# VectorE makes both low halves of a weight unit from the fourth z unit on; GpSimd keeps the inputs of the scan and the roots

## The reference, cut to what matters

```python
proj = h @ w_in
z, xBC, dt_raw = split(proj, [D_INNER, D_INNER + CONV_DIM])   # z: 2048 wide
xBC = silu(causal_depthwise_conv(xBC)); xs, Bm, Cm = split(xBC)
dt = softplus(dt_raw + dt_bias); cum = cumsum(dt * A)         # per head, 32 heads
L = exp(where(causal, cum[t] - cum[s], -inf))
y = sum_s (C_t . B_s) * L[t, s] * dt_s * x_s + D_skip * x     # 4 groups of 8 heads
y = y * silu(z); y = y * rsqrt(mean(y * y) per group + eps) * g_out
h = h + y @ w_out                                             # w_out: 2048 x 1024
```

## Time and profile before

| what | before |
|---|---|
| median of three runs | 934.71 us |
| the profiled execution | 935.1 us |
| its span, first to last instruction | 933.3 us |
| TensorE products busy | 911.1 us (98%) |
| VectorE busy | 607.2 us (65%) |
| ScalarE busy | 473.8 us (51%) |
| GpSimd busy | 123.1 us (13%), 100 instructions |
| second halves: VectorE L1744, GpSimd L2436 | 106, 21 |
| mean granted TensorE clock | 0.998 |

### The profile page before, as it was taken

How to read it: one execution, slowest core, us unless ns; L and a number is a source line. 1 busy time by engine, 2 the same in 40 slices (tenths; PEclk the granted TensorE clock), 3 DMA queues, 4 the chain that set the end, 5 groups by cost and what they waited for, 6 DMA issues and landing times.

```text
span 933.3 us, 13488 instructions
## 1 busy us (share of the span) xinstructions
PE 911.1 (98%) x4978; PEld 767.0 (82%) x4978; DVE 607.2 (65%) x1071; ACT 473.8 (51%) x764; POOL 123.1 (13%) x100
## 2 busy tenths in 40 slices
PE   9999999999999999999999999999999999999996
PEld 7999878889888869887888888877978788888885
DVE  4898677676668585767664545567486965555445
ACT  5855757466686444762543443325574354334330
POOL 5643863102000010002000000000001100000001
PEclk9999999999999999999999999999999999999999
DMA  9655232663533128232475555544432265555521
GB/s 351 231 183 169 95 124 86 224 227 137 188 128 136 57 68 338 91 112 116 156 261 182 180 201 199 172 150 163 154 136 91 95 226 213 175 193 180 184 87 45
DMA packets 22235, 151.72 MB, mean 163 GB/s; under 512 B 2592, under 2 KB 2976, under 8 KB 4256
## 3 DMA queue, kind: packets, MB, share of 16 engines
q1 hardware_dynamic: 20160, 142.62, 42.8%
q10 hardware_dynamic: 2016, 8.29, 2.3%
HBM read 149.85 MB, written 1.05 MB: 162 GB/s over the span
## 4 chain that ended last, share of the span: by engine, by line
PE 85%; DVE 8%; issue 3%; ACT 3%; POOL 1%; POOLq 0%; DVEq 0%; ACTq 0%
PE ps L492 15%; PE ps L494 15%; PE ps L498 15%; PE ps L1091 5%; PE ps L523 3%; PE ps L527 3%; PE ps L525 3%; PE ps L767 2%; PE ps L769 2%; PE ps L768 2%; PE ps L543 2%; PE ps L1109 2%; PE ps L663 2%; PE ps L666 1%; PE ps L665 1%
## 5 line engine op out<-in xcount | busy, mean ns | idle before, releaser
L1273 ACT CAST whi<-raw 128x2048 fp32r<-128x2048 f32 (+1 forms) x127 | 241.3, 1906 | 145.2 <-PE ps L498 112.6
L1738 DVE TENSOR_TENSOR wlo<-raw,whi 128x1024 fp32r<-128x1024 f32 x127 | 167.3, 1317 | 139.2 <-ACT whi L1273 138.8
L492 PE MATMUL ps<-whi,ahi 128*128 128x512 f32 (+2 forms) x448 | 173.6, 388 | 0.8 <-issue 0.6
L494 PE MATMUL ps<-wlo,ahi 128*128 128x512 f32 (+2 forms) x448 | 171.7, 383 | 0.0
L498 PE MATMUL ps<-whi,alo 128*128 128x512 f32 (+2 forms) x448 | 170.8, 384 | 0.0
L1744 DVE TENSOR_TENSOR wlo<-raw,whi 128x1024 fp32r<-128x1024 f32 x106 | 129.2, 1219 | 0.0
L492 PEld LDWEIGHTS ps<-whi,ahi 128*128 128x128 f32 x448 | 84.1, 188 | 18.5 <-issue 2.5
L498 PEld LDWEIGHTS ps<-whi,alo 128*128 128x128 f32 x448 | 84.1, 188 | 16.5
L494 PEld LDWEIGHTS ps<-wlo,ahi 128*128 128x128 f32 x448 | 84.2, 188 | 16.3 <-issue 0.5
L523 PE MATMUL ps<-ahi,whi 128*128 128x256 f32 x256 | 73.2, 286 | 0.0
L525 PE MATMUL ps<-alo,whi 128*128 128x256 f32 x256 | 72.4, 283 | 0.0
(11 more groups left out here) (282 smaller groups left out, 1710.2 us busy)
## 6 DMA issues: line engine op xcount, KB each, us to landing
raw<-in_wstream SPq DMA_DIRECT2D x134, 1024.0 KB, 4.8
par<-in_params ACTq DMA_DIRECT2D x5, 1024.0 KB, 4.8
tab<-in_tables ACTq DMA_DIRECT2D x1, 1370.0 KB, 9.0
res<-in_x SPq DMA_DIRECT2D x2, 512.0 KB, 4.6
out<-res SPq DMA_DIRECT2D x4, 256.0 KB, 2.0
par<-in_params ACTq DMA_DIRECT2D x1, 512.0 KB, 3.7
arena<-in_wf ACTq DMA_DIRECT2D x2, 256.0 KB, 5.1
arena<-in_wsmall ACTq DMA_DIRECT2D x1, 256.0 KB, 8.6
```

The costliest lines, as they stand in the source:

```text
L492: pe.matmul(banks[b][:, 0:cw], h_, wh[:, i, c], start=st, stop=False, skip_group_check=True)
L494: pe.matmul(banks[b][:, 0:cw], h_, wl[:, i, c], start=False, stop=False, skip_group_check=True)
L1273: act.copy(whi[:, u % SPL, c], raw[:, u % RAW, c]).then_inc(w_hi, 1)
L1738: dve.tensor_tensor(wlo[:, u % SPL, c], raw[:, u % RAW, c], whi[:, u % SPL, c].bitcast(F32), ALU.subtract).then_inc(w_lo_v, 1)
```

## The change

One line. `WHOLE_FROM` goes from unit 21 to unit 15:

```diff
-WHOLE_FROM = ("ssm_out", 1)
+WHOLE_FROM = ("z", 3)
```

## The result

The changed kernel takes 943.45 us (median of four runs, 943.40 to 945.03) against 934.75 for the kernel before (median of its four): 8.7 us or 0.97% longer, ratio 1.0097 with a 95% interval of 1.0086 to 1.0109. The forecast was 942.3, in a range of 938.3 to 944.3. The profiled execution took 943.4 us with a span of 941.6 (before 935.1 and 933.3).

What follows compares the result with a forecast made beforehand. TensorE was taken to bound the kernel, each stop in the scan lasting to the end; 1.11 + 2.61 + 1.6 + 1.14 + 1.14 = 7.6 us on 934.71 gave 942.3 us, range 938.3 to 944.3.

Steps and rivals of the forecast that it cites:

- place 1: Units 15 and 16, ahead of `bound(2)`: VectorE 4.0 us late, 2.9 hidden by TensorE's lead, +1.11 us.
- GpSimd's relief: GpSimd loses some 14 us of work; claimed worth nothing by itself, as TensorE waits for none of its halves.
- The lock goes to and fro: VectorE's SBUF halves and GpSimd's operations exclude each other and alternate; chance 0.68, 942.3 us.
- The rival of unparted halves: VectorE makes its two halves without GpSimd between: 938.6 us; chance 0.23, including parted at some places only.
- place 2: Unit 17 at pair 4, meeting GpSimd's inputs of group 2: TensorE restarts at 121.72 instead of 118.00, +2.61 us here.
- place 5: Unit 20 at pair 15, ahead of `y_out(3)`, gate products and norms before TensorE's turn of y: +1.14 us.
- place 3: Unit 18 at pair 8, meeting GpSimd's inputs of group 3: `mixw(9)` 1.93 us late, +1.6 goes on.
- place 4: Unit 19 at pair 11: `mixw(12)` comes one half later and TensorE waited there already, +1.14 us.
- about 1.1 near 111: TensorE's wait at L689 for `mixw` near 111 us in the changed profile, named beforehand as about 1.1 us.
- near 133: TensorE's wait at L689 for `mixw` near 133 us in the changed profile, named beforehand as 1.7 us.
- The clock: Rival: TensorE's clock falls to 1.2 GHz behind new stalls; two such places give some 947 us; chance 0.04, another late wait included.

Runs made afterwards that it cites:

- the spread halves: Changed kernel with units 17 to 19 cut into single halves put where VectorE waits for exponentials; 936.04 us.
- filled: Changed kernel with 11 unused products added on TensorE at p = 5, ahead of the L689 that waits longest; 942.02 us.
- l17: Kernel before, with both halves of units 17 to 20 on VectorE, units 15 and 16 shared as before; 940.71 us.
- l18: Kernel before, with both halves of units 18 to 20 on VectorE; 938.65 us.
- lock: Changed kernel with GpSimd's inputs of groups 1, 2 and 3 held back until VectorE made both halves of units 16, 17 and 18; 938.79 us.
- l19: Kernel before, with both halves of units 19 and 20 on VectorE; 937.07 us.

## Why the prediction was right, and what it missed

*TensorE bounds, and a wait in the scan stays to the end.* Right: the lateness of 8.69 us at the turn of y is still 8.3 at the end, and the 0.4 between them is found in other kernels' traces too.

*The order of the scan is a chain through VectorE and ScalarE with TensorE beside it.* Right: at place 1 TensorE's lead hid 2.9 of 4.0 us, as forecast, at the other four nearly all of VectorE's lateness came through, and the spread halves, on the same engine in the same number, cost almost nothing at places 2 to 4.

*GpSimd's relief is worth nothing, its earlier inputs cost.* Right: with its inputs held back the time fell by 4.7 us.

*The lock goes to and fro, operation by operation.* Right in every turn seen; a half took 2.06 us wherever a whole GpSimd operation got in ahead of it. By the rule of the Trainium skill that I cited for it (SBUF — State Buffer, Who interferes with whom) the loser blocks for the whole instruction, and the trace agrees: 2.06 is 1.22 and most of a GpSimd operation of 1.04. The rival of unparted halves gave 938.6, and the kernel in which they are nearly all unparted took 938.79. (A side remark of the prediction is not right for the kernel before: GpSimd's inputs of group 2 start there at 116.21, right behind its own half, and wait for no `y_out`; in the changed kernel they do, for 6.99 us.)

*Terms.* Place 1 1.07 for 1.11, place 2 2.62 for 2.61, place 5 1.13 for 1.14. The forecast for place 3 was a little short (1.6, measured 1.74 in "filled") and that for place 4 a little long (1.14, measured 0.93); together 2.74 for 2.67. At place 3 I had gone by the chain and not by TensorE: `mixw(9)` at 128.83 would have let it restart at 129.56 and it started at 129.74, so it was itself the later one by 0.18, and 1.93 less 0.18 is 1.75. Of the waits named beforehand, "about 1.1 near 111" was the lateness and not the wait (0.51), and "near 133" does not follow from the prediction's own sum, which gives 129.74 + 5.3 = 135.0.

*The clock.* This was the term missing from the forecast, as I had put it aside as a rival with a chance of 0.04, two such places and 947 us. It came at one place and cost 1.2 to 1.4 us, which is the whole of the forecast's error of 1.15: the wait of 2.7 us was foreseen, and that no row showed what such a wait does was said, but from waits of 1.0 us at full clock I took it as nearly excluded. Without it ("filled") the time is 942.02, against 942.3. That 943.45 lies inside the range is luck in part: its upper end had room for one more GpSimd operation of 1.0 us, which did not come, and the clock took up that room.

## What to carry to other kernels

What a moved operation costs is read where it will stand in its new engine's queue: the same six halves cost 8.7 (the clock's 1.2 to 1.4 among them), 4.1 or 1.4 us by their places and by who asks for the lock between them. Look for the wait that ends last at that place, and for gaps in which the engine waits for another; a busy share of 65% tells nothing of either. Where a chain already makes TensorE wait, give work to the idle engine rather than take it from there, and do not let a helper engine's burst start at the same signal as the critical engine's SBUF work.

## What the hardware did that I had not expected

Behind a wait of 2.7 us the granted clock fell to 1.2 GHz for products until about 127 us (0.85 and 0.53 in the two stretches); behind waits of 1.8 us (l17), 1.6 us (l18), 1.3 us ("lock") and a wait of the same place cut to 0.24 us by filler ("filled") it stayed at 1.00. Whether it falls at this place in each execution, these runs do not tell: each kernel has one trace, and single executions of the changed kernel (945.03), of l18 (941.06) and of l19 (938.83), with mean clocks of 0.994 or 0.995, and two of l17, with 0.997, are 1.1 to 2.5 us longer than the shortest of the same kernel, without a trace to show why. Idle filler on TensorE, 11 products, made the whole kernel 1.4 us faster than the changed one. The price of the fall was also partly given back: with TensorE slow, VectorE made up some of its lateness, and the wait at place 3 was 1.13 us instead of 1.57 ("filled").
